# Attention by head groups with the projections inside it, out projection last, and an expert list of 17 weight slots written out

## What is computed

```python
hp_n = rms_norm(hp, norm_mix[i])                     # hs: the 32 sample rows, likewise
# layer 0: 16 query heads of 64, 4 K/V heads, window of 128, sinks, ALiBi
o = sink_attend(qc, kb, vb, bias, valid, sinks);  y = o.reshape(b_, t, 1024) @ w_o
# layer 1: 8 heads, two softmax maps of 64 each, full cache
p = jax.nn.softmax(s, axis=-1);  a = p[:, :, 0] - lam * p[:, :, 1]
y = (rms_norm(a @ v, subln) * (1.0 - lam_init)).reshape(b_, t, 1024) @ w_o
hp = hp + yp
# 32 experts in 4 groups of 8: the best group, then its two best experts
hp = hp + hier_moe(rms_norm(hp, norm_ffn[i]), w_route_group[i], ..., w_gate[i], w_up[i], w_down[i])
```

## Time and profile before

| | us |
|---|---|
| median of 3 runs (lowest, highest) | 1339.78 (1334.65, 1341.63) |
| the profiled execution | 1337.06 |
| its span from the first to the last instruction | 1335.3 |
| PE busy in it | 1089.4 |
| mean granted TensorE clock | 0.905 of full speed |

### The profile page before, as it was taken

One profiled execution on the slowest core, in us unless ns is written; L12 is line 12 of the kernel. 1 busy time (PEld: TensorE's weight loads), 2 busy tenths in 40 slices (PEclk: granted clock), 3 DMA queues, 4 the chain that ended last, 5 costly groups with the idle time before them and its releaser, 6 DMA issues.

```text
span 1335.3 us, 18796 instructions
## 1 busy us (share of the span) xinstructions
PE 1089.4 (82%) x6824; PEld 780.4 (58%) x6824; DVE 385.8 (29%) x1296; ACT 245.9 (18%) x736; POOL 317.9 (24%) x571
## 2 busy tenths in 40 slices
PE   4998899969987788649999988987777899788840
PEld 3886688755554455338888766665564455454520
DVE  2011555461111111160011245553171211111115
ACT  2000633301110110020110144432101011011101
POOL 4101322222322222121000023322023223222213
PEclk8999899959999999959999999998768889999985
DMA  9212000379999999592103222000088999999934
GB/s 308 64 63 95 1 1 1 123 291 374 375 393 393 392 393 397 211 345 86 63 0 129 78 83 87 12 1 19 29 332 309 355 347 389 390 390 390 358 131 182
DMA packets 81189, 279.78 MB, mean 210 GB/s; under 512 B 10734, under 2 KB 37438, under 8 KB 63392
## 3 DMA queue, kind: packets, MB, share of 16 engines
q1 hardware_dynamic: 63440, 231.75, 45.9%
q0 software_dynamic: 15840, 35.96, 7.8%
q10 hardware_dynamic: 1840, 11.14, 2.2%
HBM read 266.54 MB, written 28.70 MB: 221 GB/s over the span
## 4 chain that ended last, share of the span: by engine, by line
PE 60%; DMA 22%; DVE 8%; issue 4%; POOL 3%; ACT 3%; SPq 1%; DVEq 0%; POOLq 0%; ACTq 0%
PE ps L1437 20%; DMA area<-in_w_up 18%; PE ps L1642 11%; PE ps L1428 9%; PE ps L1654 5%; PE ps L1624 3%; PE ps L1829 2%; PE ps L1587 1%; DVE area L930 1%; PE ps L1603 1%; PE ps L1445 1%; PE ps L1571 1%; POOL small L678 1%; SPq L410 1%; ACT area L899 1%
## 5 line engine op out<-in xcount | busy, mean ns | idle before, releaser
L1437 PE MATMUL ps<-ring,xT 128*128 128x256 f32 (+1 forms) x1184 | 283.4, 396 | 5.7 <-DVE hid L1009 4.7
L1437 PEld LDWEIGHTS ps<-ring,xT 128*128 128x128 f32 (+1 forms) x1184 | 227.7, 197 | 44.1 <-DVE hid L1009 5.2
L1642 PE MATMUL ps<-ring,area 128*64 128x256 f32 x512 | 129.9, 412 | 33.5 <-DMA ring<-in_w_up 21.6
L1642 PE MATMUL ps<-area 128*64 128x256 f32 x496 | 124.2, 408 | 39.9 <-DMA area<-in_w_up 27.2
L589 POOL DMA_INDIRECT y_scratch<-area,cur_i x64 | 65.3, 1020 | 341.7 <-DVE area L1176 308.7
L1643 PE MATMUL ps<-ring,area 128*64 128x256 f32 x512 | 130.2, 412 | 0.0
L1643 PE MATMUL ps<-area 128*64 128x256 f32 x496 | 124.7, 409 | 0.0
L1428 PE MATMUL ps<-xT,ring 128*128 128x272 f32 x512 | 121.6, 401 | 0.9 <-ACT xT L737 0.9
L1163 DVE TENSOR_TENSOR area<-area,ps 64x256 f32<-64x256 f32 x64 | 27.2, 425 | 308.2 <-ACT area L807 308.2
L1642 PEld LDWEIGHTS ps<-ring,area 128*64 128x64 f32 x512 | 73.2, 148 | 72.0 <-issue 33.6
L1428 PEld LDWEIGHTS ps<-xT,ring 128*128 128x128 f32 x512 | 99.6, 195 | 22.3 <-ACT xT L737 1.0
(11 more groups left out here) (224 smaller groups left out, 1386.9 us busy)
## 6 DMA issues: line engine op xcount, KB each, us to landing
area<-in_w_down SPq DMA_DIRECT2D x33, 1024.0 KB, 19.6
ring<-in_w_gate SPq DMA_DIRECT2D x32, 1024.0 KB, 21.3
ring<-in_w_up SPq DMA_DIRECT2D x32, 1024.0 KB, 24.4
ring<-in_w_down SPq DMA_DIRECT2D x32, 1024.0 KB, 20.8
area<-in_w_gate SPq DMA_DIRECT2D x31, 1024.0 KB, 23.2
area<-in_w_up SPq DMA_DIRECT2D x31, 1024.0 KB, 23.6
ring<-in_w_b_qkv SPq DMA_DIRECT2D x12, 1024.0 KB, 10.8
area<-y_scratch ACTq DMA_DIRECT2D x8, 1024.0 KB, 8.2
```

Source lines behind the costliest of these rows:

```text
L1437: ins = nc.tensor.matmul(ps[:r, bank, 0:F], xT[:, k, COL[t]:COL[t] + r], ring_k(n)[:, k, :], start=k == 0, stop=k == KD - 1)
L1642: nc.tensor.matmul(ps[0:CAP, bank, 0:F], x[:, k, :], wg[:, k, :], start=k == 0, stop=k == KD - 1)
```

## The change

Attention of both layers is ordered by heads: unit u is head group u // 5 and tile LATE[u % 5], with LATE = [4, 3, 2, 1, 0].

- Layer 0: K and V of a tile are computed as soon as that tile is normed (`kv_a`); x is loaded in five pieces; the Q halves of the next head group are computed between the steps of the present one (`q_a`).
- Layer 1: the K, V and Q of two heads (a pair) are 14 "positions" (`POS`). Those of pair 0 stand before the loop and use four PSUM banks, those of pair p + 1 stand between the steps of pair p, three to a step, and all use bank 7 alone, which ACT or DVE empties after each. The two heads' probabilities are double-buffered. K is transposed for the next position's use (L2064). The sample rows' K and V are a position of each pair.
- Out projection: an item may be the first six of eight 128-row blocks, the last two, or all eight. `out_items` gives their order; the first fourteen or five stand in the last head group, where no more projections are left, the others after the loop, with the flips, logits and routing of a tile among them.
- Experts: all 32 are written out. The weights go through one list of 17 slots, load n after load n - 17 has been used. The overfull expert's weights are loaded, and it is run, after expert 29. Gathers and scatters read the index table directly; the buffers are not cleared. POOL loads the next gain and layer 1's cache rows and tables right behind the experts.
- SP's loads of layer 1's attention weights no longer wait for the scattered rows.

The core of the diff:

```diff
+def pair_positions(p):
+    k = [("K", t, t - 1 if t else None) for t in range(4)]
+    v = [("V", t, None) for t in range(4)]
+    rest = [("KS", None, 3), ("F", None, None)]
+    q = [("Q", (m, h), 4 if (m, h) == (0, 0) else None) for m in range(2) for h in range(2)]
...
+            out.append(Pos(p, main, arg, flip, 7, i % 3 == 0 or main == "KS" or (main, arg) == ("K", 2)))
...
+MOE_SLOTS = [["R4", "R5"] + FREED + ["R0", "R1", "R2", "R3", "N0", "N1", "X0", "X1"],
...
+NSLOT = len(MOE_SLOTS[0])
...
+        def position(n):
+            x = POS[n]
+            pb = x.pair % 2
+            same = [i for i in range(n) if POS[i].bank == x.bank]
+            if same:
+                emptied, count = (pos_dve, POS_DVE) if POS[same[-1]].dve else (pos_act, POS_ACT)
+                pe.wait_ge(emptied, count[same[-1]])
...
+        for step in range(UNITS):
+            scores_b(step)
+            if step >= 2:
+                turn_out(step - 2)
+            pos_at(step, 0)
+            if step >= 1:
+                turn_b(step - 1)
+            pos_at(step, 1)
+            if step >= 1:
+                values_b(step - 1)
+            pos_at(step, 2)
...
-            for x in xg:
-                ins = nc.gpsimd.memset(x, 0.0)
...
+            x_transpose(0)
+            for e in range(NE):
+                gate_up(e)
+                if e + 1 < NE:
+                    x_transpose(e + 1)
+                if e:
+                    down(e - 1)
+                h_transpose(e)
...
-                if i == 1:
-                    sp.wait_ge(y2_in[0], 16)
-                    sp.wait_ge(y2_in[1], 16)
```

More of the change, by code:

```diff
@@ L12 @@
+from collections import namedtuple
 from contextlib import ExitStack
@@ L45 @@
 B_HEADS, BHD = 8, 128
+PAIRS = B_HEADS // 2
 SCALE = HD ** -0.5
@@ L337, in o_item, with weights, last_use @@
-    def o_item(layer, step):
-        i = step - (7, 8)[layer]
-        return i if 0 <= i < O_ITEMS - 1 else None
+    def weights(key):
+        name, value = WHERE[key]
+        return part(slot_at[name], SLOT), w_ready[name], value
+    def last_use(key):
+        kind, x, i = key[0], key[1], key[2]
+        if kind == "e":
+            return (d_mm if key[3] == 2 else gu_mm), NE * x + i + 1
+        if x == "o":
+            return o_mm, OUT_BASE["ab".index(kind) + 1]
+        if kind == "a":
+            return (q_mm, 4 * i + 4) if x == "q" else (kv_mm, NT)
+        reads = {"k": "K KS", "v": "V KS", "q": "Q"}[x].split()
+        return pos_mm, 1 + max(n for n, s in enumerate(POS) if s.pair == i and s.main in reads)
@@ L593, in moe @@
-            half = NE // 2 * layer
-            def step(turn, u, last=False):
-                e = DEEP * turn + u
-                if not last:
-                    pool.wait_ge(x_flip, NE * layer + e + 1)
-                    gather(e + DEEP, u)
-                before = half + DEEP // 2 * turn + u // 2
-                first = isinstance(turn, int) and turn == 0 and u < 2
-                scatter(e, u % 2, None if first else 16 * before)
-            for u in range(DEEP):
-                gather(u, u)
@@ L789, in moe @@
         def moe(layer):
-            norm(1 + 2 * layer, range(EARLY, NT))
             act.wait_ge(r_exp, layer + 1)
@@ new lines, in pos_act_at @@
+        def pos_act_at(step, place):
+            n = step_pos(step, place)
+            if n is not None and not POS[n].dve:
+                pos_act_copy(n)
+        for step in range(UNITS):
+            if step >= 2:
+                o_copy(step - 2)
+            exps("b", b_unit, E_B[step % 2], step)
+            if step >= 1:
+                b_flip_copy(step - 1)
+            pos_act_at(step, 1)
+            if step == UNITS - 1:
+                square(3, 0)
+            if step >= 1:
+                o_squares(step - 1)
+            pos_act_at(step, 2)
@@ L902, in _ @@
+        o_copy(UNITS - 2)
+        xt_copy(3, 0)
+        b_flip_copy(UNITS - 1)
+        square(3, 1)
+        o_squares(UNITS - 1)
+        xt_copy(3, 1)
+        o_copy(UNITS - 1)
+        for i in range(2, NT):
+            square(3, i)
+            xt_copy(3, i)
         moe(1)
-        norm(4)
+        for i in range(NT):
+            square(4, i)
     @block.vector
@@ L987, in bias_max, with route_clear @@
+        kv_copy_a(4)
+        q_copy(0, 0)
+        q_copy(0, 1)
+        def route_clear():
+            nc.vector.memset(lg, 0.0)
+            nc.vector.memset(both, 0.0)
+            nc.vector.memset(gtop, 0.0)
+            nc.vector.memset(etop, 0.0).then_inc(r_clear, 1)
+        def bias_max(layer, unit, E, u, bank, tab):
             t, j, kc, nk, tc, vt = unit(u)
@@ L1482, in route_before @@
             r = ROWS[t]
[L1483 to L1489 removed]
+            pe.wait_ge(r_hot, NT * layer + i + 1)
@@ new lines, in _ @@
+        for step in range(UNITS):
+            j, i = divmod(step, NT)
+            scores_a(step)
+            if step >= 3:
+                values_a(step - 3)
+            if step >= 2:
+                turn_a(step - 2)
+            if j < 3 and i < 4:
+                q_a(j + 1, i // 2, i % 2)
+            if j == 3 and i == 0:
+                out_item(0, 4)
+            if j == 3 and i >= 1:
+                out_item(0, 3, s=i - 1)
+        values_a(UNITS - 3)
+        out_item(0, 4, part2=True)
@@ new lines, in _ @@
+        for step in range(UNITS):
+            scores_b(step)
+            if step >= 2:
+                turn_out(step - 2)
+            pos_at(step, 0)
+            if step >= 1:
+                turn_b(step - 1)
+            pos_at(step, 1)
+            if step >= 1:
+                values_b(step - 1)
+            pos_at(step, 2)
+        flips(3, 0)
+        turn_out(UNITS - 2)
+        out_item(1, 1, s=2)
+        turn_b(UNITS - 1)
+        logits(1, 0)
+        out_item(1, 1, s=3)
+        values_b(UNITS - 1)
@@ L1847, in _ @@
+        route_slots(1, 2)
+        logits(1, 3)
+        out_item(1, 0, s=3)
+        route_before(1, 3)
+        route_slots(1, 3)
+        flips(3, 4)
+        logits(1, 4)
+        route_before(1, 4)
+        route_slots(1, 4)
         moe(1)
```

2265 lines of the change are left out of this document (1249 added, 1016 removed).

## The result

The changed kernel takes 1306.33 us (median of 4 runs, 1299.61 to 1308.57) against 1339.53 before: a ratio of 0.976, 95% interval 0.974 to 0.979. It is faster by 33 us; 106 were forecast, and the time lies above the range of 1195 to 1285. The profiled execution took 1305.91 and its span is 1304.1.

A forecast was written before the change was run, and what follows sets the result against it. PE was taken to bound attention and weight loads most of the experts; gains of 24 + 17 + 36 + 29 = 106 from 1337.1 gave 1231, plus 2.7 for the median: 1234 us. Range 1195 to 1285.

The forecast's parts named there:

- I keep 10 of the 39.3: Layer 1's attention: ordering by heads cuts PE's gaps from 39.3 us to 10.
- Four of five tiles have 20 us or more of out items left over them: Before the experts, both layers: argument against long tails, that out items remain to cover four tiles' picks.
- 335.8: Layer 1's attention: PE's busy time of 335.8 us, carried over from the kernel before.
- What stays is 21.5: Last out item to first gate product, both layers: 38.9 us in layer 0 falls to 21.5, one tile's chain.
- The term of 2.9 for the memset: Before the experts: a pick slowed while POOL cleared buffers; without the clearing 2.9 us goes.
- 77 loads x 2.96: Layer 0's experts: 77 loads after the first 19, 2.96 us each, 227.9; stage 252.2, a gain of 17.
- Layer 1's experts: Layer 1's expert stage: 80 loads x 2.96, overfull expert among the others; 289.7 to 261.1 us, a gain of 29.
- one bank: Rival, layer 1's attention: 42 positions each wait 1.6 us for one PSUM bank, 67 in all; 1291 us, chance 0.13.
- Long tails: Rival, before the experts: DVE can't do picks beside residuals, both 38.9 us stay; 1269 us, chance 0.11.
- The weights come no sooner: Rival, expert stages: prefetch fills the same slots as before, 46 us don't come; 1280 us, chance 0.07.
- Experts by PE: Rival, expert stages: weights stay ahead, PE bounds; stages 216 and 223 us plus 10; 1180 us, chance 0.05.
- code that stalls: Rival, experts: fetching unrolled code through full DMA engines, 5.9 us at every fourth expert; 1535 us, chance 0.04.

The follow-up runs named there:

- e4: Changed kernel with layer 1's tail in another order on POOL, DVE and PE, same instructions: 1278.51 us.
- e10: Changed kernel with five expert loads of layer 0, and two of layer 1, waiting for the last out item: 1300.53 us.
- e5: Changed kernel with 70 extra matmuls, results unused, where PE waits in layer 1's tail: 1296.84 us.
- e9: Changed kernel with the edits of e2, e3 and e4 together: 1268.40 us, ratio to the kernel before 0.947.
- e3: Changed kernel with four expert loads (slots N0, N1, X0, X1) also waiting for the first gather: 1295.31 us.
- e11: Changed kernel with POOL's clearing of the four gather buffers put back: 1301.73 us.
- e2: Changed kernel with layer 1's attention weights, from the second load on, held until the first two tiles of scattered rows are in: 1299.93 us.
- e1: Changed kernel with half of each expert matrix after the first 17 of a layer not loaded: 1226.64 us in one run.
- e7: Changed kernel with one DVE swap in layer 0: last quarter of tile 0's residual ahead of the pick of tile 1's experts: 1306.69 us.
- e8: The changed kernel itself run again, without an edit: 1307.39 us.

## Why the prediction was wrong

The direction was right, and so were most parts of attention. The forecast missed by 74 us of span (1230.3 to 1304.1): 4.5 to the first gate product of layer 0, 17.0 in its experts, 35.0 in layer 1's attention, 15.9 in its experts, 1.4 at the end. The steps that failed:

- **"I keep 10 of the 39.3" (layer 1's gaps).** This is the largest. PE's work to the last out item was 358.5 (291.98 + 66.48), against a sum of 355.7. The gaps were 31.6: 13.1 up to the end of the loop, close to the 10, and 18.5 in the tail. I had reckoned with PE's load alone and not with DVE's and POOL's written order in the tail, where picks stand ahead of residuals and the heads' norms ahead of a tile's. "Four of five tiles have 20 us or more of out items left over them" was the sentence that failed: in layer 0, with more items behind the loop, the same picks are hidden (PE busy 225.25 of 232.40); in layer 1, with ten items left, they are not. e4 shows it: another order alone takes 28 us out of this stretch.
- **The clock was missing in the sum.** PE's 66.48 us in that tail are 51.37 in e4 and 59.21 in e10, for the same matmuls, and e5 shows that filling the waits with useless work pays. The sum didn't ask at which clock a stretch would run: its 335.8 came from a row at 0.94, while the loop ran at 1.00 and the tail at 0.78. That work and sum agree to 2.8 us is therefore luck, and so in part is e9's 409.7: its work is some 12 us below the sum's, its gaps some 9 above the 10.
- **"What stays is 21.5" (before the experts): 28.8 and 30.1.** The step was to take four picks and the clearing out of a chain that ran through DVE, and to leave the rest as it was. With the picks gone the chain runs through the last tile's flips and logits on PE, which the 21.5 names but takes from no row. 4.7 and 3.3 us of what is over are the gathers, 8.45 and 7.08 instead of 3.74: of the eight loads that were issued from 249.97 on, the last still run beside the first gather; e3 gives it its 3.54 back and brings layer 0's first gate product to 274.7. Some 1.9 us in each layer are the last tile's logits, which come after waits of PE; the tile before had them at a clock near full:

```profile
241.25 1.71 PE ps L1727 x16
...
256.51 3.62 PE ps L1727 x16
```

In layer 1 the last tile's scale also stands behind a pick (1.0 us), and its flips behind the list products of the tile before (1.8). These three are read from the rows and no run tested them; they would leave some 0.6 us in each layer. The term of 2.9 for the memset is worth nothing in layer 0 of the changed kernel, where no pick falls into it (e11); in layer 1 the clearing costs the chain 4 us, which a shorter gather hid. In layer 0 a last out item 2.8 us sooner than forecast covers part of the miss: PE's work was 7.4 below the sum, the first projection 2.5 later and the gaps 2.1 more.
- **"77 loads x 2.96": 252.2 was 269.2.** The last scatter took 3.4 more, beside layer 1's weights (e2). The rest, 13.6, has two parts. The first is the price, which was read too low. I took 63 loads for the 186.5 us from 372.9 to 559.4; the queues' view of the kernel before has for SP's there (q1: packets, MB, share)

```profile
q1 hardware_dynamic: 12437, 64.72, 88.9%
```

A load is 1.049 MB, so these are 61.7 loads, 3.02 us each, and from 312.1 to 559.4 (85.36 MB) it is 3.04. The changed kernel kept that pace. From 292.8 to 366.4 its queue has

```profile
q1 hardware_dynamic: 4326, 24.28, 88.8%
```

and from 366.4 to 520.0:

```profile
q1 hardware_dynamic: 9668, 54.25, 92.3%
```

These are 23.2 loads by 3.18 us and 51.7 by 2.97, 3.03 in the mean: 5.5 us more than by 2.96. The second part is that loads land behind their bytes: by 520 the queue had moved 93.9 of 96 loads, but the 92nd (the row "496.37 26.56") landed at 522.9, while I let each land when its bytes were due, some 8 us. The price could have been tried on the kernel before: there 15.6 loads had moved 14.1 us into the stage, so the rule gives 14.1 + 80.4 x 2.96 + 10.2 = 262, and 269 with 3.04; the stage took 269.0.
- **What the 17 slots were worth.** The changed kernel has 17 loads in at the first gate product, the one before had 12, and the stage is as long. e3 and e10 show why the lead is not kept: the eighteenth load needs a slot that expert 0 frees, so the DMA engines are at 0.46 for 14.1 us, and a kernel that loads less ahead fills just that time. That idle time was in my sum; that the kernel before didn't have it (0.78 there) was not held against the gain.
- **Layer 1's experts** are 277.0 and not 261.1. Beyond e1, no run took this stage apart; that the reasons are those of layer 0 is argued from the like size of the miss, 16 and 17. What was gained, 13 of the 29, is the overfull expert: before, the stage was 20.7 longer than layer 0's, now it is 7.8 longer.

The rivals: one bank did not stall (5 us of waits, 67 forecast). Long tails came true in part, not by DVE's load as I put it but by the order in layer 1's last out items (e4); before the experts 28.8 and 30.1 stay of the 38.9. "The weights come no sooner" came true for layer 0 in its result, though 17 loads were in. Experts by PE fell (269.2 and not 226), and so did code that stalls: 6.76 us an expert with the DMA engines at 1.02 (292.8 to 366.4). That rival's turning point counts 8.3 us an expert where its next sum counts 8.0; with 8.0 it is 9.7 and not 10.0.

The Trainium skill's rule on taking turns between queues (DMA: Bandwidth & Descriptors, Queues, rings and completion order) agrees with the scatter and the gathers here: 6.63 and 8.45 us beside weight loads, 2.87 and 3.54 without. For the row load an estimate by it, 4.82 doubled, is 9.6; 8.23 was measured, and 7.29 with the weights held back and POOL's queue still beside it, at shares of 46.0% and 50.5%.

## What to carry to other kernels

A stage that is bound by bytes is priced from its first byte to its last landing, by a pace tried on the trace at hand, and a prefetch counts only if the transfers don't stand still behind it for the slots it has filled. Work that is moved into a loop's tail needs its order on every engine looked at, not PE's load alone: an in-order engine that does a long pick ahead of the step that empties a bank stops PE, and the lower clock makes the wait dearer than it is long. An early transfer is not free: look at which small transfer on the chain it will run beside. And an edit that changes no time may hold two effects that cancel, as e11 did: read its rows.

## What was not expected of the hardware

PE did 70 matmuls more and the kernel was 10 us faster, with the mean granted clock in that stretch at 0.93 instead of 0.78. The tail of layer 1 takes 85.0 us at a clock of 0.78 in the changed kernel, e3, e7 and e8, and 78.3 to 81.8 at 0.81 to 0.85 in e1, e2, e10 and e11, whose edits don't touch it, with gaps of 18.2 to 19.1 us in all eight; this alone moves the time by 3 to 7 us. A DVE step of 0.49 us took 4.45 while POOL cleared buffers. And in layer 0's expert stage the changed kernel moves 384 GB/s between 400 and 500 us where the one before moved 393, at the same share of the DMA engines, 1.02; why was not found.
